# Between two layers: the context rows finished first, and the next layer's context keys, values and latents made beside the latent tiles

## The reference

```python
for l in range(DEPTH):
    ctx_out = l < DEPTH - 1
    mod_l = jnp.split((silu_c @ ada_w[l] + ada_b[l])[:, None, :], N_MOD, axis=-1)
    mod_c = jnp.split(silu_cc @ ada_w[l] + ada_b[l], N_MOD, axis=-1)
    h_l = modulate(rmsnorm(x, norm_mix_pre[l]), mod_l[0], mod_l[1])
    h_c = modulate(rmsnorm(ctx, norm_mix_pre[l]), mod_c[0], mod_c[1])
    m_l, m_c = mix_heads(h_c, h_l, ...)
    x = x + mod_l[2] * rmsnorm(m_l, norm_mix_post[l])
    ...
    f_l = expert_choice_ffn(modulate(rmsnorm(x, norm_ffn_pre[l]), mod_l[3], mod_l[4]), ...)
    x = x + mod_l[5] * rmsnorm(f_l, norm_ffn_post[l])
    if ctx_out:
        f_c = expert_choice_ffn(modulate(rmsnorm(ctx, norm_ffn_pre[l]), mod_c[3], mod_c[4]), ...)
        ctx = ctx + mod_c[5] * rmsnorm(f_c, norm_ffn_post[l])
```

## Time and profile before

| what | us |
|---|---|
| median of 3 runs | 2176.77 (2176.59 to 2177.65) |
| span of the profiled execution | 2177.5 |
| PE busy in it | 1918.7 (88%) |
| DVE busy | 634.1 (29%) |
| ACT busy | 505.1 (23%) |
| POOL busy | 206.9 (10%) |

### The profile page before, as it was taken

How to read it: one execution, slowest core, us unless ns; L and a number is a source line. 1 busy time by engine, 2 the same in 40 slices (tenths; PEclk the granted TensorE clock), 3 DMA queues, 4 the chain that set the end, 5 groups by cost and what they waited for, 6 DMA issues and landing times. The chain is left out here.

```text
span 2177.5 us, 25201 instructions
## 1 busy us (share of the span) xinstructions
PE 1918.7 (88%) x10588; PEld 917.6 (42%) x10588; DVE 634.1 (29%) x1197; ACT 505.1 (23%) x1000; POOL 206.9 (10%) x225
## 2 busy tenths in 40 slices
PE   5988999979889999999995999999694987778776
PEld 2656555534423333333333766655342333222222
DVE  2257542362431111111105256523523100000002
ACT  3145541452200000000014145514321100000001
POOL 2300000210011011111011000001100100000000
PEclk9999999999989999999997999999796999889898
DMA  9520304111389999999997123014318999999996
GB/s 346 171 78 2 136 1 181 52 56 64 116 318 399 397 394 401 394 394 402 395 379 285 39 78 136 1 58 175 130 54 322 393 397 405 401 400 406 401 400 265
DMA packets 166913, 534.52 MB, mean 245 GB/s; under 512 B 11208, under 2 KB 19730, under 8 KB 166802
## 3 DMA queue, kind: packets, MB, share of 16 engines
q1 hardware_dynamic: 148720, 487.40, 57.5%
q0 software_dynamic: 16416, 40.21, 6.5%
q10 hardware_dynamic: 1666, 5.31, 0.6%
HBM read 507.98 MB, written 24.90 MB: 245 GB/s over the span
## 5 line engine op out<-in xcount | busy, mean ns | idle before, releaser
L2807 PE MATMUL ps<-ring,arena 128*64 128x512 f32 x1040 | 252.2, 640 | 49.3 <-DMA ring<-in_w_up 46.2
L2807 PE MATMUL ps<-arena 128*64 128x512 f32 x816 | 188.2, 611 | 27.6 <-DMA arena<-in_w_up 27.6
L2146 PE MATMUL ps<-arena,ring 128*128 128x256 f32 (+1 forms) x640 | 201.7, 477 | 5.6 <-DVE arena L1413 5.6
L2807 PEld LDWEIGHTS ps<-ring,arena 128*64 128x64 f32 x1040 | 80.8, 147 | 208.0 <-issue 204.2
L2146 PEld LDWEIGHTS ps<-arena,ring 128*128 128x128 f32 x640 | 122.7, 193 | 85.3 <-issue 69.9
L2064 DVE TENSOR_TENSOR arena<-arena,ps 128x512 f32<-128x512 f32 x32 | 22.0, 688 | 431.9 <-ACT arena L1317 431.9
L2655 PE MATMUL ps<-ring,arena 128*128 128x512 f32 x320 | 141.3, 595 | 1.0 <-ACT arena L1272 0.6
L1317 ACT ACTIVATE arena<-ps 128x512 f32<-128x512 f32 x32 | 19.1, 598 | 456.1 <-PE ps L2807 456.1
L2807 PEld LDWEIGHTS ps<-arena 128*64 128x64 f32 x816 | 61.2, 141 | 143.8 <-issue 143.8
L2854 PE MATMUL ps<-ring,arena 128*64 128x512 f32 x496 | 111.1, 594 | 1.4 <-ACT arena L1342 1.4
L2854 PE MATMUL ps<-arena 128*64 128x512 f32 x480 | 107.7, 594 | 2.9 <-DMA arena<-in_w_down 2.2
(11 more groups left out here) (366 smaller groups left out, 2472.3 us busy)
## 6 DMA issues: line engine op xcount, KB each, us to landing
ring<-in_w_up SPq DMA_DIRECT2D x33, 2048.0 KB, 16.4
ring<-in_w_gate SPq DMA_DIRECT2D x32, 2048.0 KB, 21.1
ring<-in_w_down SPq DMA_DIRECT2D x31, 2048.0 KB, 23.0
ring<-in_ada_w SPq DMA_DIRECT2D x24, 2048.0 KB, 12.3
arena<-in_w_down SPq DMA_DIRECT2D x21, 2048.0 KB, 23.5
arena<-in_w_gate SPq DMA_DIRECT2D x19, 2048.0 KB, 20.1
arena<-in_w_up SPq DMA_DIRECT2D x18, 2048.0 KB, 15.0
ring<-in_w_in SPq DMA_DIRECT2D x6, 2048.0 KB, 17.7
```

The source lines that it names most:

```text
L2146: ins = mm(o[0:n, c0:c1], w[:, k, col:col + n], hT[:, k, c0:c1], start=k == 0, stop=k == KD - 1)
L2807: ins = mm(px[0][hf * 64:hf * 64 + 64, col:col + 512], xl[e % 2][:, at:at + CAP_L], w[c][:, hf * 512:hf * 512 + 512], start=b + c == 0, st ...
```

## The change

Sums: POOL's indirect adds of the context and of the latent rows are separated (`add_context_rows`, `add_latent_rows`), and the last expert's context add stands before the latent add of expert 14. POOL, not ACT, loads the sums back: the two context tiles as soon as the context is summed up, the four latent tiles after the phase. PE's last three down products are reordered (`last_downs`), so that the context comes first; the context gate row and the parameters are made before the last latent down product, and three of the four `ada_w` blocks before the phase. DVE makes both diagonals for the gates at the start of expert 15, and takes layer 1's parameters before the phase.

Between the layers ACT and DVE finish tiles 0 and 1 first, modulate them, and go on to the tiles 2 to 5. PE meanwhile turns the two context tiles and makes their keys, values and latents (`context_of_layer`), then turns the latent tiles, all four for one feature block at a time (`latent_rows_of_layer`). The queries, keys and values that follow are then for latent tokens alone. Some buffers move, and the job numbers with them.

```diff
-                ctx_on = l < DEPTH - 1
+            def add_context_rows(l, e):
                 if l == 0 and e == 0:
                     pool.wait_ge(s_fzero, 16 * stored(DEPTH - 1))
                 if e:
+                    pool.wait_ge(put_ctx, 16 * (l * NE + e))
+                pool.wait_ge(S["y_ctx"], l * NE + e + 1)
+                pool.indirect_dma_start(quarters_sum[l], at_rows(e, NE), y_c[e % 2], None, compute_op=ALU.add)\
+                    .then_inc(put_ctx, 16)
+            def add_latent_rows(l, e):
+                if e:
                     pool.wait_ge(put_lat, 16 * (l * NE + e))
-                    if ctx_on:
-                        pool.wait_ge(put_ctx, 16 * (l * NE + e))
-                if ctx_on:
-                    pool.wait_ge(S["y_ctx"], l * NE + e + 1)
-                    pool.indirect_dma_start(quarters_sum[l], at_rows(e, NE), y_c[e % 2], None, compute_op=ALU.add)\
-                        .then_inc(put_ctx, 16)
                 pool.wait_ge(S["y_lat"], l * NE + e + 1)
                 pool.indirect_dma_start(halves_sum[l], at_rows(e, 0), y_l[e % 2], None, compute_op=ALU.add)\
                     .then_inc(put_lat, 16)
...
-                        add_rows(l, e - 4)
+                        if l < DEPTH - 1:
+                            add_context_rows(l, e - 4)
+                        if l < DEPTH - 1 and e - 4 == NE - 2:
+                            add_context_rows(l, NE - 1)
+                        add_latent_rows(l, e - 4)
...
+                def load_sums(t):
+                    pool.dma_start(Fa[:, t, :], sum_hbm[l][t * P:(t + 1) * P, :]).then_inc(x_back[t], 16)
                 if l < DEPTH - 1:
-                    add_rows(l, NE - 1)
+                    pool.wait_ge(S["gu_lat"], NE * (l + 1))
+                    pool.wait_ge(put_ctx, 16 * NE * (l + 1))
+                    for t in range(CT):
+                        load_sums(t)
+                    add_latent_rows(l, NE - 1)
                 phase()
+                if l < DEPTH - 1:
+                    pool.wait_ge(put_lat, 16 * NE * (l + 1))
+                    for t in range(CT, NT):
+                        load_sums(t)
                 if l + 1 < DEPTH:
...
+                if ctx_on:
+                    copy_out(GBf[l][1], J.tile(last_gate_job(l, 1))[:, :], last_gate_job(l, 1))
                 weighted(NE - 1)
...
-                if ctx_on:
-                    load_sums(n0 + NE)
-                    for s in range(streams(l)):
-                        copy_out(GBf[l][s], J.tile(jb("gf") + s)[:, :], jb("gf") + s)
...
                 if ctx_on:
-                    act.wait_ge(S["coef_ready"], l + 2)
-                    turned_out(0)
-                    residual(q[-1])
-                    turned_out(2)
-                    turned_out(4)
+                    summed(0)
+                    summed(1)
+                    residual(0)
+                    rows_out(l + 1, 0)
+                    residual(1)
+                    columns_out(l + 1, 0)
+                    copy_out(GBf[l][0], J.tile(last_gate_job(l, 0))[:, :], last_gate_job(l, 0))
+                    context_turned_out()
+                    for t in range(CT, NT):
+                        summed(t)
+                        if t > CT:
+                            residual(t - 1)
+                    residual(NT - 1)
+                    j = JOB[l + 1, "kc"]
+                    act.wait_ge(*J.filled(j))
+                    for m in range(2):
+                        ins = context_heads_out(KH, m, J.tile(j)[:, 512 * m:512 * m + CTX], 1.0)
+                    ins.then_inc(*J.free(j))
+                    context_latents_out(l + 1)
+                    latents_turned_out(0)
+                    latents_turned_out(2)
+                else:
+                    for t in q:
+                        summed(t)
...
+                    if ctx_on and e == NE - 1:
+                        for s in (1, 0):
+                            TT(diagf[s], ident.unsqueeze(1).to_broadcast([P, KD, P]),
+                               cGf[:, :, s].unsqueeze(2).to_broadcast([P, KD, P]), ALU.mult).then_inc(S["diag_ready"], 1)
...
+                    weighted(NE - 2)
                     weighted(NE - 1)
-                dve.wait_ge(S["down_lat"], n0 + NE)
-                for s in range(streams(l) if ctx_on else 0):
-                    TT(diagf[s], ident.unsqueeze(1).to_broadcast([P, KD, P]),
-                       cGf[:, :, s].unsqueeze(2).to_broadcast([P, KD, P]), ALU.mult).then_inc(S["diag_ready"], 1)
...
                     dve.wait_ge(s_late, 16 * N_LATE)
                     parameters(l + 1)
...
-                    turned_out(1)
-                    normed(q[-1])
-                    turned_out(3)
-                    turned_out(5)
+                if ctx_on:
+                    normed_and_summed(0)
+                    normed_and_summed(1)
+                    normed(0)
+                    normed(1)
+                    first_modulation(l + 1)
+                    context_turned_out()
+                    for t in range(CT, NT):
+                        normed_and_summed(t)
+                        if t > CT:
+                            normed(t - 1)
+                    normed(NT - 1)
+                    j = JOB[l + 1, "vc"]
+                    dve.wait_ge(*J.filled(j))
+                    dve.tensor_copy(V[:, 0:CT, :].rearrange("p t n -> p (t n)"), J.tile(j)[:, 0:256 * CT]).then_inc(*J.free(j))
+                    latents_turned_out(1)
+                    latents_turned_out(3)
...
+            def latent_rows_of_layer(j):
+                for b in range(4):
+                    pe.wait_ge(*J.empty(j + b))
+                    for i in range(2):
+                        k = 2 * b + i
+                        for t in range(CT, NT):
+                            if k == 0:
+                                next_rows_ready(t)
+                            at = i * SEQ + (t - CT) * P
+                            ins = pe.transpose(J.tile(j + b)[:, at:at + P], Fa[:, t, k * P:(k + 1) * P], ident)
+                    ins.then_inc(*J.fill(j + b))
...
+            def context_of_layer(l, wb):
+                context_rows_of_layer(JOB[l, "hc"])
+                w, j = arrived(wb + 4), JOB[l, "kc"]
+                pe.wait_ge(*J.empty(j))
+                for m in range(2):
+                    for k in range(KD):
+                        if m == 0 and k % 4 == 0:
+                            pe.wait_ge(*J.freed(JOB[l, "hc"] + k // 4))
+                        ins = mm(J.tile(j)[:, 512 * m:512 * m + CTX], w[:, k, (2 + m) * P:(3 + m) * P], hT[:, k, 0:CTX],
+                                 start=k == 0, stop=k == KD - 1)
+                ins.then_inc(*J.fill(j))
+                w = arrived(wb + 5)
+                token_major(JOB[l, "vc"], w[:, :, 0:256], range(CT), 256, 256)
+                w, lc = arrived(wb + 6), latent_start(l, 0)
+                pe.wait_ge(s_dtw, 16 * (l + 1))
+                token_major(JOB[l, "lc"], w[:, :, lc:MLA_COLS + 16], range(CT), MLA_COLS + 16 - lc, 512, lc)
...
-                    normed_rows_turned(jb("h"))
+                    context_of_layer(l, wb)
+                    latent_rows_of_layer(jb("hl"))
...
-                    feature_major(jb("qk") + m, w, m * P, P, t0 if m < 2 else 0,
-                                  ready=first_h if l == 0 and m == 0 else None)
+                    feature_major(jb("qk") + m, w, m * P, P, t0,
+                                  ready=(latents_ready if l else first_h) if m == 0 else None)
...
                 w = arrived(wb + 5)
-                token_major(jb("v"), w[:, :, 0:256], range(0, 4), 256, 256)
-                token_major(jb("v") + 1, w[:, :, 0:256], range(4, 6), 256, 256)
+                if l:
+                    token_major(jb("v"), w[:, :, 0:256], range(CT, NT), 256, 256)
+                    pe.wait_ge(*J.freed(jb("kc")))
+                    pe.wait_ge(*J.freed(jb("vc")))
...
                 map_scores(0)
                 block_rows(l, 1, 0)
                 w = arrived(wb + 6)
-                pe.wait_ge(s_dtw, 16 * (l + 1))
-                lc = latent_start(l, 0)
-                token_major(unit("latents", 0), w[:, :, lc:MLA_COLS + 16], range(2), MLA_COLS + 16 - lc, 512, lc)
+                if l == 0:
+                    pe.wait_ge(s_dtw, 16)
+                    token_major(unit("latents", 0), w[:, :, 0:MLA_COLS + 16], range(CT), MLA_COLS + 16, 512)
...
+                def last_downs():
+                    n = BLOCKS[l].index((2, NE - 2, 0))
+                    context_hidden_turned(NE - 1)
+                    context_down_ready(NE - 2)
+                    w = [block(n), block(n + 1)]
+                    context_down(NE - 2, 0, w[0])
+                    context_down(NE - 2, 1, w[1]).then_inc(S["down_ctx"], 1)
+                    latent_down_ready(NE - 2)
+                    latent_down(0, w[0]).then_inc(S["blocks_used"], 1)
```

(26 more changed lines are left out.)

212 lines of the change are left out of this document (111 added, 101 removed).

## The result

The changed kernel takes 2165.68 us (median of 5 executions, 2162.41 to 2171.14) against 2176.77 us (5 executions, 2176.37 to 2180.67); the ratio is 0.9943, 95% interval 0.993 to 0.9956. It is faster, by 11 us (0.6%) where 21.2 were predicted, and outside the predicted range of 2150 to 2163. Its profiled execution has a span of 2166.7 us, and its own time is 2168.7: spans lie about 2 us under times. By that estimate the profiled execution of before (span 2177.5) was one of about 2179.4 us, and not 0.7 us above the median, as the prediction had it.

The account below looks back on a forecast made before the run. It took engines, not transfers, to bound the seam between the layers, with six tiles in a row on DVE. First map 17.9 us earlier plus 3.3 at its turning gave 21.2: 2176.8 - 21.2 = 2155.6 us, range 2150 to 2163.

Parts of the forecast that it names:

- 1: last down product later: At the seam, half the gate rows and the parameters' transpose move ahead; last down product ends 1.3 us later, at 1148.3.
- 2: gates and modulation's blocks, from that product on: PE runs three `ada_w` blocks, half the gates, the fourth block: 8.9 us, to 1157.2; no delay taken, 3 us as bound.
- 3: from there to the context's keys: Two context tiles are normed, modulated and turned first; the context's keys start at 1164.6, counted 1163.6, at the latest 1166.3.
- 4: the moved products: Context's keys, values and latents run beside the latent tiles' norms: 19.0 us plus 2.0 for the clock, ending at 1185.6.
- 5: 32 transposes, slack of ACT and DVE: Latent tiles end at 1181.6, about 4 us to spare; transposes take 4.7, queries and keys start at 1190.3.
- 6: queries and keys to the first map: Shorter products of layer 1, 27.8 + 3.4 + 13.9 + 1.2; first map starts at 1236.6, 17.9 us earlier.
- 7: first map to its turning: Latents no longer stand between layer 1's maps; first map turned after 8.0 us, before 11.32, saving 3.3 (1.5 to 5.0).
- Rival B: Context chain late: fourth block or keys' weights +2.9, low clock +2, slow latent transposes +2.0; 2162.5 us; chance 0.20.
- C: Latent sum loads, moved to POOL's queue, come late at the seam: 2157.2 us; chance of a real loss 0.04.
- D: Seam gets shorter but the end does not, since transfers of layer 1's experts set it: 2176.8 us; chance 0.03.
- E: More gain: context keys at 1163.6 (-1.0), no clock loss (-2.0), latents' removal in full (-1.7): 2150.9 us; chance 0.10.

## Why the prediction was wrong

By its own steps, measured from the end of the last down product (1156.54), where the prediction's frame had 1148.3:

| step | predicted | measured |
|---|---|---|
| 1: last down product later | 1.3 | 1.1 |
| 2: gates and modulation's blocks, from that product on | 8.9 | 13.7 |
| 3: from there to the context's keys | 7.4 | 7.6 |
| 4: the moved products | 21.0 | 20.3 |
| 5: 32 transposes, slack of ACT and DVE | 4.7, 4 | 3.5, 4.6 |
| 6: queries and keys to the first map | 46.3 | 46.5 |
| 7: first map to its turning | 8.0 | 7.9 |

**Step 2 is the step that failed.** It put the wait for the fourth block at nothing, and the wait was 3.30 us. The prediction had all the numbers: the slot comes free one product before the end, the load takes 13.9 us. It landed where those say: requested at 1153.15, there at 1167.05. By the prediction's own frame that is 1158.5 against a need at 1157.2 less the block's own 1.8, so about 3 us late, and it took 0, because the loads ahead were spaced wider. That spacing did not shorten this one. The block behind the wait ran at 1.2 GHz, 3.19 us in place of 1.9. These two are 4.6 of the 4.8 us of the table. The same wait was 2.84 to 3.80 us in all six profiles. Steps 4 and 5 gave 1.9 back: of the 2.0 us for the clock 1.3 were needed in this profile (and none in the other five), and the transposes ran at 0.109 us each. Rival B's mechanism, the fourth block, was real, with the context's keys 5.0 us late where B had 2.9, and its 2162.5 comes nearer to the result than the forecast; but a late block alone is not the result. Nor do the runs show that the 4.8 us could be had back: the edits that shortened or filled the wait left the seam within its spread.

**The rest lies outside the sum.** The first pair's seams differ by 142.0 - 123.6 = 18.4 us, 2.8 short of 21.2. Five profiles put the seam of before at 140.2: the one that I summed from was on the long side, and that takes 1.3 more. Of the remaining 17.1, 1.8 went in the first maps, 2.0 in layer 0 and 0.5 later. That leaves 12.8 in the profiles, 12.0 in the means of all executions, and 11.1 between the two medians first measured. So of the 10.1 us between forecast and result 2.8 lie in the sum's own steps, 1.3 in a long seam of before, 4.3 in stretches that the sum did not cover, and 1.7 in which executions were drawn. The prediction treated step 7 as a pure gain and did not ask what the clock does when the latents' cover goes. It charged clock losses on the context's products (2.0), where 1.3 came in one profile of six, and none behind the maps. And it had no term for stages that the change does not touch, though one execution was all that it had of them.

**The rivals.** C falls, since ACT and DVE had slack: POOL's six loads (L907, in two groups) landed in 6.6 to 9.9 us, where ACT's six in one group had taken 5.6 to 12.9. Source line L907 of after:

```profile
DMA to landing us min/median/max: 6.6/8.3/9.9
```

The four latent loads were issued from 1167.21 on, 10.7 us after the last down product where the prediction had 8.7; they waited for the last indirect add, which began at 1158.22 and landed 8.4 us later.

The Trainium skill, "SBUF — State Buffer", section "SBUF: two separate sides", has VectorE shut GpSimd out of writing descriptors in some of its operations. This run hardly tests that: DVE ran one scaling of 0.76 us at 1167.17 and then stood idle until 1172.51, while POOL issued the four loads between 1167.21 and 1169.64. D falls as it was put: the profiles after the first maps differ by 0.5 us, and no transfer takes the gain back. E's premise, no loss to the clock, held for the context's products in five of six profiles (not in the first), and not for the block and the maps.

## What to carry to other kernels

When a load is requested at a known event and takes a known time, put its landing beside the need and charge the difference; do not set it to zero because its neighbours got easier. When an operation moves out of a gap that another engine's work makes, the gap is left bare, and on TensorE the price may appear behind it, as a lower clock on work that was not changed (here 81.8 to 82.1 us in place of 77.9 to 82.8). A wait that is filled or ended can pass its price on in the same way: the context's keys took 8.7 to 9.2 us in place of 7.14. And where single executions of a kernel differ by as much as half the gain, take several profiles of both before summing stages: the changed seam here was steady to 1 us, the seam of before only to 3.7, and the stretch ahead of them moved by up to 11.6.

## What the runs showed of the hardware

The granted clock fell from 2.4 to 1.2 GHz at 235 us in three profiles with PE busy in all of the 4.00 us ahead (the window 230 to 234 above) and in the following 14, and did not in others with the same instructions. The fall cost 6.2 us each time. The Trainium skill, "TensorE: Matmul & The Clock Gate", section "What's actually happening" of Part 1, ties the clock to how busy PE has been. Busy time as the profile counts it does not tell these executions apart. Elsewhere the time of one stage moved from execution to execution too: layer 0's stretch from the first product of L2474 (now L2570) to the first of L2624 (now L2720) took 109.7 to 115.5 us, while the experts' latent gate and up products, from first to last, took 500.8 us in each of the nineteen profiles.
